# Two attention beginnings in a new order of waits, copies and roundings

## The reference

```python
def mla_mixer(xn, w_in, q_norm, w_uq, kv_norm, w_ukv, w_o, cos_r, sin_r):
    c = xn @ w_in                                    # 384 + 256 + 32 columns
    cq = rms_norm_2(c[..., :384], q_norm)            # query latents: 3 tiles of 128
    ckv = rms_norm_2(c[..., 384:640], kv_norm)       # key/value latents: 2 tiles
    kr = c[..., 640:]                                # one rotated key part for all heads
    qf = (cq @ w_uq).reshape(B, S, 16, 64 + 32)
    q_rope = apply_rope(qf[..., 64:], cos_r, sin_r)
    kv = (ckv @ w_ukv).reshape(B, S, 16, 64 + 64)
    k_rope = broadcast(apply_rope(kr))
    o = causal_attention(concat(qf[..., :64], q_rope), concat(kv[..., :64], k_rope), kv[..., 64:])
    return o.reshape(B, S, 1024) @ w_o
```

## Time and profile before

| | |
|---|---|
| median of the runs | 1141.34 us (1139.76 to 1141.94, 3 runs) |
| the profiled execution | 1140.0 us, span of its instructions 1138.2 us |
| PE busy | 1113.8 us, 98% of the span |
| DVE, ACT, POOL busy | 872.7, 712.6 and 88.8 us |
| mean granted TensorE clock | 0.993 of full speed; 1.00 in both stretches of the change |
| second attention with its values | about 548 to 640 us of the span |
| latent attention, from its latents on | about 843 to 945 us |

### The profile page before, as it was taken

The page is one execution under the profiler, slowest core; times in us unless marked ns, Lnnn a source line. Parts: engine busy times, 40 slices in busy tenths (PEclk is TensorE's granted clock), DMA queues, the critical chain, the costliest instruction groups (busy, mean ns, idle before and its releaser), DMA issues.

```text
span 1138.2 us, 25181 instructions
## 1 busy us (share of the span) xinstructions
PE 1113.8 (98%) x9391; PEld 1076.8 (95%) x9391; DVE 872.7 (77%) x1640; ACT 712.6 (63%) x1296; POOL 88.8 (8%) x141
## 2 busy tenths in 40 slices
PE   9998999999999999999989999999999999999997
PEld 8998999988999999999889999999998889999997
DVE  6888878686578998888778588777777858876774
ACT  7768764476646666655699476555565836655553
POOL 0000000065200000000023100000001420000000
PEclk9998999999999999999999999999999999999999
DMA  7665645531373776666545357666653425776661
GB/s 250 195 207 185 185 126 164 170 112 57 91 207 130 208 225 195 191 195 186 166 150 148 101 158 221 206 192 195 190 153 102 130 87 164 214 217 191 194 192 37
DMA packets 52780, 190.28 MB, mean 167 GB/s; under 512 B 5984, under 2 KB 6240, under 8 KB 52704
## 3 DMA queue, kind: packets, MB, share of 16 engines
q1 hardware_dynamic: 52272, 188.11, 54.5%
q10 hardware_dynamic: 432, 1.12, 0.3%
HBM read 188.16 MB, written 1.05 MB: 166 GB/s over the span
## 4 chain that ended last, share of the span: by engine, by line
PE 85%; DVE 5%; ACT 5%; DMA 2%; issue 2%; SPq 0%; DVEq 0%; ACTq 0%
PE bank L619 25%; PE bank L621 24%; PE bank L620 24%; PE bank L738 2%; DMA w_raw<-weight_stream 2%; DVE w_low L1804 2%; PE bank L750 2%; ACT w_high L1301 1%; PE bank L627 1%; PE bank L629 1%; PE bank L628 1%; PE bank L767 1%; ACT h_high L1344 1%; ACT arena L1661 1%; PE bank L765 1%
## 5 line engine op out<-in xcount | busy, mean ns | idle before, releaser
L1301 ACT ACTIVATE w_high<-w_raw 128x1024 fp32r<-128x1024 f32 x355 | 374.1, 1059 | 262.6 <-PE bank L621 169.5
L1804 DVE TENSOR_TENSOR w_low<-w_raw,w_high 128x1024 fp32r<-128x1024 f32 x355 | 433.0, 1223 | 132.0 <-ACT w_high L1301 130.2
L619 PE MATMUL bank<-h_high,w_high 128*128 128x256 f32 x1760 | 494.4, 281 | 1.0 <-DVE w_low L1804 0.4
L621 PE MATMUL bank<-h_high,w_low 128*128 128x256 f32 x1760 | 487.4, 277 | 0.0
L620 PE MATMUL bank<-h_low,w_high 128*128 128x256 f32 x1760 | 487.4, 277 | 0.0
L619 PEld LDWEIGHTS bank<-h_high,w_high 128*128 128x128 f32 x1760 | 331.2, 188 | 6.2 <-issue 2.1
L620 PEld LDWEIGHTS bank<-h_low,w_high 128*128 128x128 f32 x1760 | 330.9, 188 | 0.0
L621 PEld LDWEIGHTS bank<-h_high,w_low 128*128 128x128 f32 x1760 | 330.6, 188 | 0.0
L619 PE MATMUL bank<-r_high,w_high 128*128 128x256 f32 x942 | 268.0, 285 | 9.3 <-DVE arena L1866 2.9
L620 PE MATMUL bank<-r_low,w_high 128*128 128x256 f32 x942 | 262.5, 279 | 0.0
L621 PE MATMUL bank<-r_high,w_low 128*128 128x256 f32 x942 | 262.4, 279 | 0.0
(11 more groups left out here) (224 smaller groups left out, 1071.9 us busy)
## 6 DMA issues: line engine op xcount, KB each, us to landing
w_raw<-weight_stream SPq DMA_DIRECT2D x355, 512.0 KB, 4.0
x<-x_in SPq DMA_DIRECT2D x4, 256.0 KB, 5.6
small<-small_in ACTq DMA_DIRECT2D x1, 937.5 KB, 4.7
out<-arena SPq DMA_DIRECT2D x3, 256.0 KB, 2.3
out<-arena SPq DMA_DIRECT2D x1, 128.0 KB, 2.5
out<-arena ACTq DMA_DIRECT2D x1, 128.0 KB, 2.6
small<-small_in ACTq DMA_DIRECT2D x1, 30.5 KB, 4.1
```

The lines of the kernel that those rows point to most:

```text
L619: mm(out_ap, wh, high, start=start, stop=False, skip_group_check=True)
L621: return mm(out_ap, wl, high, start=False, stop=stop, skip_group_check=True)
L1301: fn(w_high[:, c % RING, :], w_raw[:, c % RAW, :], ACT.Copy).then_inc(high_ready, 1)
L1804: v.tensor_tensor(w_low[:, c % RING, :], w_raw[:, c % RAW, :], f(w_high[:, c % RING, :]), ALU.subtract).then_inc(low_ready, 1)
```

## The change

It changes the order of instructions on PE, ACT and DVE, and adds one instruction:

- Second attention: the load of Exp's table moves from behind the value stage to ahead of it, right behind `roots(2)`. The rounding of the chunk six behind the last value chunk moves from ahead of the first `rope_halves` to behind it, and each of the next ones one item later (`behind=1`); behind the third item two are rounded. DVE's low halves follow the same order.
- Latent attention, PE: the wait for the last latent tile's copy moves from ahead of the value stage to behind its first six matmuls (`inside_values`).
- DVE: `turn_key` moves ahead of `latent_inverse(0)`. Of the four `values_out`, number 0 goes to ACT, behind the first two key copies; a new semaphore `first_values` orders it, and `acc_read` gets two counts from the last copy of DVE.
- ACT: a dummy loads Exp's table ahead of `query_copy(0)`; the chunks `ukq`+4 and +5 are rounded behind `query_copy(0)` and `query_copy(2)`, ahead of all exponents, and on DVE at heads 0 and 1 of the attention.
- `LATENT_SPLITS` is now one chunk a block: `ukq`+6+q at head 2q+1 on ACT and 2q+2 on DVE.
- Each dummy of a table load writes a column of its own in `stats`.

```diff
@@ -383,6 +383,7 @@
         c_rstd_ready = sem("latent_rstd_ready")
         c_spread = sem("latent_rstd_spread")
         c_normed = sem("latent_normed")
+        first_values = sem("first_quarter_of_values_copied")
         k2_ready = sem("mla_rotated_keys_spread")
         keys_done = sem("mla_key_products")
         queries_done = sem("mla_query_products")
...
@@ -459,16 +460,7 @@
                 eng.wait_ge({"k": keys_done, "q": queries_done}[kind],
                             sum(not ends_chunk(kind, j) for j in range(i + 1)))
-        def latent_splits():
-
-            out, at = collections.defaultdict(list), -1
-            for q in range(-SIZE["uv"], SIZE["ukq"]):
-                kind, i, _ = UNITS[max(8 * q + 7, 0)]
-                at = max(at + 1, 2 * i - 3 if kind == "k" else i - QUERIES_AHEAD)
-                out[at].append(BASE["ukq"] + q + RING)
-            return out
-
-        LATENT_SPLITS = latent_splits()
+        LATENT_SPLITS = {2 * q: BASE["ukq"] + q + RING for q in range(SIZE["ukq"])}
         QK_AHEAD = 3
...
@@ -1188,12 +1180,12 @@
                         latent_root_spread(1)
             column_tiles("c2", h_high, h_low, inside=inside_latents, norm=4)
-            tile_read(pe, "c2", 5)
             pe.wait_ge(std_ready, 5)
             pe.wait_ge(c_normed, 2)
             def inside_values(k, t):
                 if (k, t) == (0, 0):
+                    tile_read(pe, "c2", 5)
                     latent_norm_sums(0)
                 if (k, t) == (1, 0):
                     latent_root_spread(0)
...
@@ -1258,8 +1250,10 @@
             def queries_keys_and_bank(h):
                 queries_and_keys(h)
-                if h < 2:
-                    pe.wait_ge(acc_read, 4 * ACC_V2 + 2 + h)
+                if h == 0:
+                    pe.wait_ge(first_values, 1)
+                if h == 1:
+                    pe.wait_ge(acc_read, 4 * ACC_V2 + 2)
             for m in range(2):
                 key_product(m)
...
@@ -1638,21 +1632,21 @@
             stage("wo", lambda i: None, DT - LATE)
             norm(1)
             late_splits(BASE["ffn0"], LATE)
-            fn(stats[:, 6:7], eps_col, ACT.Sqrt)
+            fn(stats[:, 9:10], eps_col, ACT.Sqrt)
             feed_forward(0)
             norm(2)
             late_splits(BASE["v1"], LAG)
             roots(2)
+            fn(stats[:, 10:11], eps_col, ACT.Exp)
             stage("v1", lambda i: None, SIZE["v1"] - 1)
             act.wait_ge(chunk_used, BASE["v1"] + SIZE["v1"])
             for p in range(4):
                 read_acc(p, v1[:, p // 2, (p % 2) * 512:(p % 2 + 1) * 512], scale=rstd_col[:, p // 2:p // 2 + 1])
-            split_high(BASE["v1"] + SIZE["v1"] - 1 + RING)
-
-            def rope_halves(n):
+
+            def rope_halves(n, behind=0):
                 act.wait_ge(chunk_used, BASE["qk1"] + n + 1)
                 if n >= 2:
                     act.wait_ge(rope_done, n - 1)
...
@@ -1661,11 +1655,12 @@
                     ins = fn(rope_swap[at:at + HD // 2, n % 2, :], qk_bank(n)[other:other + HD // 2, :], ACT.Copy,
                              scale=qk_scale(n))
                 ins.then_inc(halves_swapped, 1)
-                split_high(BASE["qk1"] + n + RING)
-
-            fn(stats[:, 7:8], eps_col, ACT.Exp)
+                split_high(BASE["qk1"] + n - behind + RING)
+
             for n in range(QK_AHEAD):
-                rope_halves(n)
+                rope_halves(n, behind=1)
+            split_high(BASE["qk1"] + QK_AHEAD - 1 + RING)
+
             def behind_block(j, part):
                 n = QK_AHEAD + 2 * j + part
...
@@ -1731,8 +1726,13 @@
             for m in range(2):
                 key_copy(m)
-            for h in range(QUERIES_AHEAD):
+            fn(v2[:, 0, 0:512], acc[0][:, :], ACT.Copy).then_inc(first_values, 1)
+            fn(stats[:, 15:16], eps_col, ACT.Exp)
+            query_copy(0)
+            split_high(BASE["ukq"] - SIZE["uv"] + RING)
+            for h in range(1, QUERIES_AHEAD):
                 query_copy(h)
+            split_high(BASE["ukq"] - SIZE["uv"] + 1 + RING)
             def inside_latent(j):
...
@@ -1746,16 +1746,15 @@
                     key_copy(j + 2)
                 if part and i + QUERIES_AHEAD < NH:
                     query_copy(i + QUERIES_AHEAD)
-                if i < NH:
-                    for c in LATENT_SPLITS[i]:
-                        split_high(c)
+                if part and i < NH:
+                    split_high(LATENT_SPLITS[i - 1])
             attention(3, NH // 2, probs2, probs_t2, LATER_BANKS, behind_latent, inside_latent, odd_copies=False)
             for k in range(DT - LATE):
                 projection_split("wo2", k)
             norm(5)
             late_splits(BASE["ffn2"], LATE)
-            fn(stats[:, 6:7], eps_col, ACT.Sqrt)
+            fn(stats[:, 13:14], eps_col, ACT.Sqrt)
             feed_forward(2)
             def squared(n):
...
@@ -2246,7 +2245,7 @@
             inverse_roots(2)
             v.tensor_tensor(c64r, par("c64"), rstd[:, :], ALU.mult)
             link(v.tensor_tensor(s64r, par("s64"), rstd[:, :], ALU.mult))
-            stage("v1", lambda i: None)
+            stage("v1", lambda i: None, count=SIZE["v1"] - 1)
             def rope(n):
                 dve.wait_ge(halves_swapped, n + 1)
...
@@ -2255,7 +2254,12 @@
                 link(v.tensor_tensor(b, rope_swap[:, n % 2, :], s64r, ALU.mult))
                 dve.wait_ge(qk_read, n + 1)
                 v.tensor_tensor((k1[:, 0, n // 2, :] if n % 2 else q1[:, n // 2, :]), a, b, ALU.add).then_inc(rope_done, 1)
-                split_low(BASE["qk1"] + n + RING)
+                if n < QK_AHEAD - 1:
+                    split_low(BASE["qk1"] + n - 1 + RING)
+                else:
+                    if n == QK_AHEAD - 1:
+                        split_low(BASE["qk1"] + n - 1 + RING)
+                    split_low(BASE["qk1"] + n + RING)
             def projection_split(name, k):
...
@@ -2323,14 +2327,14 @@
                 if i == 1:
                     latent_inverse(1)
                     inverse_roots(4)
+            turn_key()
             latent_inverse(0)
-            turn_key()
             latents_normed(0, 2, 5)
             split_low(BASE["c2"] + SIZE["c2"] - 1 + RING)
             dve.wait_ge(chunk_used, BASE["uv"] + SIZE["uv"])
-            def values_out(p):
-                v.tensor_copy(v2[:, p // 2, (p % 2) * 512:(p % 2 + 1) * 512], acc[p][:, :]).then_inc(acc_read, 1)
+            def values_out(p, banks=1):
+                v.tensor_copy(v2[:, p // 2, (p % 2) * 512:(p % 2 + 1) * 512], acc[p][:, :]).then_inc(acc_read, banks)
             def query_rope(h):
                 product_done(dve, "q", h)
...
@@ -2340,18 +2344,20 @@
             values_out(2)
             query_rope(0)
             query_rope(1)
-            values_out(0)
             values_out(1)
             query_rope(2)
-            values_out(3)
+            dve.wait_ge(first_values, 1)
+            values_out(3, banks=2)
             def behind_latent(j, part):
                 i = 2 * j + part
                 if i + QUERIES_AHEAD < NH:
                     query_rope(i + QUERIES_AHEAD)
-                for c in LATENT_SPLITS[i - 2]:
-                    split_low(c)
+                if i < SIZE["uv"]:
+                    split_low(BASE["ukq"] - SIZE["uv"] + i + RING)
+                if i - 2 in LATENT_SPLITS:
+                    split_low(LATENT_SPLITS[i - 2])
             attention(3, NH // 2, probs_t2, LATER_BANKS, behind_latent, odd_copies=True)
             for k in range(DT - LATE):
```

More of the change, by code:

```diff
@@ L1413, in step @@
                         roots(2 * n + 1)
-                        fn(stats[:, 7:8], eps_col, func)
+                        fn(stats[:, 44 + n:45 + n], eps_col, func)
                     if j:
@@ L1456, in _ @@
             split_high(3)
-            fn(stats[:, 6:7], eps_col, ACT.Sqrt)
+            fn(stats[:, 7:8], eps_col, ACT.Sqrt)
             split_high(4)
@@ L1529, in _ @@
             rx(RT - 1)
-            fn(stats[:, 6:7], eps_col, ACT.Sigmoid)
+            fn(stats[:, 8:9], eps_col, ACT.Sigmoid)
             def branch_gates():
@@ L1684, in _ @@
             late_splits(BASE["ffn1"], LATE)
-            fn(stats[:, 6:7], eps_col, ACT.Sqrt)
+            fn(stats[:, 11:12], eps_col, ACT.Sqrt)
             feed_forward(1)
@@ L1704, in latents_high @@
                     fn(r_high[:, LATENTS[n], :], c_norm[:, LATENTS[n], :], ACT.Copy).then_inc(latent_high, 1)
-            fn(stats[:, 6:7], eps_col, ACT.Sqrt)
+            fn(stats[:, 12:13], eps_col, ACT.Sqrt)
             for i, e in enumerate(C2_ORDER):
@@ L1769, in weighted @@
                 ins.then_inc(out_scaled, 1)
-            fn(stats[:, 6:7], eps_col, ACT.Sqrt)
+            fn(stats[:, 14:15], eps_col, ACT.Sqrt)
             squared(0)
```

## The result

The changed kernel takes 1134.12 us in the median of 6 runs (1132.91 to 1138.09), the kernel before 1141.01 us beside it (6 runs, 1139.76 to 1142.29): a ratio of 0.995 with a 95% interval of 0.9938 to 0.9962. Timed once more it was 1133.36 against 1139.58 us, ratio 0.995 (0.9934 to 0.9967). Forecast was 1135.1. The profiled execution of the changed kernel took 1134.8 us, with a span of 1133.0.

A forecast was written before the change was run, and what follows sets the result against it. PE was taken as the bound, so only its waits in the two stretches could be won: 1.05 + 5.1 = 6.15 us off 1140.0 gives 1133.8, and the median 1.3 above gives 1135.1; range 1132.3 to 1138.3.

The forecast's parts named there:

- Second attention, 1.05: Second attention: earlier table load and later roundings bring ACT's first exponents forward, winning 1.05 us of 3.7 to be had.
- The values, "1.0 us won": Latent attention: the values' first products start at 861.05 instead of 862.03, before the last tile's copy, winning 1.0 us.
- Low half 2 against POOL's fourth copy: Latent attention: DVE's low half (868.24) gets in before POOL's copy (868.27), so query 0 starts at 870.7, 1.6 us earlier.
- rival 1: Latent attention: POOL's fourth copy gets in ahead of DVE; 5.1 us won in all, 1136.2 us; chance 0.21.
- Turning the key early: Latent attention: turning the key inside DVE's idle time starts POOL's four copies at 865.0 instead of 867.49.
- First exponents at 876.15: Latent attention: ACT's chain of copies, table load and roundings lets the exponents start at 876.15, 2.25 us earlier.
- Waits left, 2.0: Latent attention: of PE's 7.1 us of waits, 0.85 (query 0), 0.4, 0.1 and 0.65 (query 6) remain; 5.1 won.
- The wait of 1.52: Latent attention: PE's long wait, from ACT stuck 2.09 us on a transfer ahead of exponents, vanishes with earlier rounding.
- The last roundings, "ACT is idle there": Latent attention's end: the last rounding moves back a block at no cost, its chunk wanted over 5 us later.
- Rival 2: Both stretches: the waits vanish nearly whole, DVE's and ACT's slack being larger; 8.8 us, 1132.5; chance 0.12.
- Rival 3: Latent attention: DVE's two low halves push the second block's maxima back; only 2.0 us won, 1139.3; chance 0.14.
- Slower by landing transfers: Second attention: later low halves delay loads; landings near 7 us would cost 8.5 us, giving 1144; chance 0.03.

The follow-up runs named there:

- e1: Kernel before with only the second attention's part of the change: 1136.69 us in one execution.
- e2: Kernel before with only the second attention's load of Exp's table moved ahead of the value stage, roundings as before: 1137.02 us in one execution.
- e3: Changed kernel with PE's wait for the last latent tile's copy put back ahead of the values: 1135.05 us in one execution.
- e8: Changed kernel with POOL's last three key copies held back behind the latents' last low half: 1134.16 us in one execution.
- e4: Changed kernel with the key turned behind the root's reciprocal again, as before: 1138.28 us in one execution.
- e6: Changed kernel with the latent attention's roundings and low halves in the old order: 1135.52 us, beside 1139.77 of before.
- e9: Changed kernel with DVE's low halves spread to one a block, ACT's order unchanged: 1133.37 us in one execution.
- e5: Changed kernel with all four quarters of the values copied by DVE, as before: 1136.37 us, beside 1139.77 of before.
- e7: Changed kernel again without edit, as a control: 1135.83 us in one execution.
- e11: Changed kernel again without edit, timed: median of 6 runs 1133.36 us, against 1139.58 of before.
- e12: Changed kernel with POOL's copies held back, one low half a block, and the second attention's roundings in before's order: median of 5 runs 1132.24 us, against 1139.58.

## Why the prediction was right

The forecast was 6.15 us, 1135.1; medians measured 6.89 and 6.22 us less than before. The stretches show 5.6 to 6.0 us. So the sum is right, within what this kernel's runs can tell, and so is the mechanism in the main: 5.6 to 6.0 us came out of PE's waits in the two stretches (5.2 to 5.8 if e1 and e2 stand for before in the latent one). One step failed, and its cost was offset by luck. The steps:

- **Second attention, 1.05.** Measured 0.97 to 1.08. First wait near 0.1: 0.16. Second about 1.5: 1.58. First exponents at 578.65: 577.50, which is 578.65 on before's clock (1.15 us ahead there). The "0.45 of waiting for PE" that the text took off the table load's 1.5 is what e2 wins back (1.50 against 1.04). The cover was there: ACT waits for no transfer between 565 and 600 us.
- **The values, "1.0 us won".** At the values' first product it is 1.01. As a gain at query 0 it is 0 to 0.4 (e3). The text named the next thing that would be late, POOL's fourth copy, but still counted the 1.0 whole.
- **Low half 2 against POOL's fourth copy.** This step failed. I took DVE to get in first, by 0.03 us; the copy did, and low half 2 took 1.26. The copies started at 864.79 on before's clock, not 865.0, and ran 1.09 apart, so the fourth began some 0.2 us sooner than I had it. That same earliness made the loss smaller than rival 1's: query 0 at 870.77, where the forecast said 870.7 and the rival 871.1. The mechanism was the rival's and the size the forecast's. So query 0's time came out right by luck. The Trainium skill's "SBUF — State Buffer", section "Who interferes with whom", says that a DVE instruction with two SBUF inputs and a reading GpSimd instruction contend, and that the order of issue decides which of them is blocked. The trace agrees: a copy under way holds off DVE's subtraction (1.26 against 0.42), and in e8 a subtraction under way isn't held off by the copy behind it (1.22 at 868.12, the copy drawn from 868.33; the three copies took 4.11 there, where one alone took 1.04).
- **Turning the key early.** Right in kind, and larger than I had weighed it: 2.0 to 2.4 us (e4), since the late copies strike all three low halves and the query chain behind. The text foretold POOL's copies "2.5 us earlier against the values"; by its own times (865.0 and 861.05, before 867.49 and 862.03) it is 1.5, and 1.7 was measured. The 2.5 is their shift on before's clock, measured 2.7.
- **First exponents at 876.15.** 876.45 on before's clock. ACT's key copies began at 870.17 and not 869.6, because its last rounding waited for DVE behind low half 2. From there to the exponents it took 6.28 us and not 6.55: successive copies and roundings are drawn overlapping by some 0.1 us (the rounding behind query copy 0, 1.05 us long from 871.91, is followed at 872.86), which the count left out. The text built this time on ACT's chain alone; by e6 DVE's maxima would not have let the exponents start before 876.46 either. That both bounds fall together is nothing that the text had worked out.
- **Waits left, 2.0.** From start to start of the matmuls, less what such a step takes without a wait, PE loses 1.0 us at query 0 (forecast 0.85), 0.2 at the first head's scores (none), 0.4 at the second head's (0.4), nothing at query 4 (0.1) and 0.7 at query 6 (0.65): 2.3. With the text's own 7.1 that makes 4.8, and the profile has 4.77. So 7.1 was right and the 2.0 was 0.3 short. The 0.2 is most likely query copy 0, which now stands behind the table load and ends at 872.01, PE going on at 872.22; the view names no cause. As idle time query 0's wait is 0.86, where about 0.7 was foretold.
- **The wait of 1.52** is gone, for the reason given (e6).
- **The last roundings, "ACT is idle there".** The text put them at nothing. The rest of the attention loses 0.15 us in the three executions of the changed kernel and in every experiment with its order of roundings, and not in e1, e2 and e6, which have before's order (0.04, 0.04 and -0.01 us gained).
- **Rival 2** (8.8 us) wasn't reached even with three repairs (7.96). **Rival 3**, given back: no; e9 shows that the two low halves cost 0.8 to 0.9 us, and the second block's exponents behind them start at 879.69 (881.81 on before's clock) where before had 883.25. **Slower by landing transfers:** no. Landings have a median of 4.2 us (4.0 in the earlier trace rows), and the second attention gained 1.0 of its 1.05.

**Open.** Behind the latent attention, from its output projection into the feed-forward, every execution loses 0.15 to 1.6 us against before's one profile, e1 and e2 among them (0.81 and 0.41), whose latent attention is unchanged. So it isn't shown to be the change's. Why the medians gain 0.2 to 1.1 us more than the stretches of the profile taken with them (6.22 against 5.97, 6.89 against 5.81) is open too; single runs of one kernel differ by 2 us and more.

## What to carry to other kernels

Where two engines shut one another out, moving one engine's work earlier is worth what the other's timetable leaves of it: find what is queued in the gap that the chain moves into, and test the two edits together and apart, since each alone may win little (here 0 to 0.4 us apart, 1.0 together). A table load moved to a place where its engine has cover was worth its whole 1.5 us here; a rounding moved away from the head of a chain partly uncovered the wait that it was hiding (0.4 to 0.5 us). Before shortening one engine's chain ahead of a step, ask which other engine that step also waits for: here ACT could take two roundings more ahead of the first exponents for nothing, since DVE's maxima weren't there sooner. If work is made ahead for one engine, ask which engine now has the matching half to do and spread that too.

## What the runs showed of the hardware

In a series of four copies of POOL the gap ahead of the last one was no opening for DVE. By the copies' even spacing (4.35 us for four) the last one began about 0.1 us before low half 2 was drawn, in the changed kernel, in e5 and in e6, and in all three low half 2 took 1.26 us in place of 0.42.

Two executions ran the same products at two paces with the same clock. Windows of 7 us in the latent attention's output projection, of before and then of the changed kernel; columns are length, busy time and count of PE, PEld, DVE, ACT and POOL, granted clock, DMA share, GB/s:

```profile
933.00:940.00 7.00, 7.00 (x64) 7.00 (x63) 4.18 (x4) 2.90 (x3) 0.00 (x0) 1.00 0.57 181
```

```profile
926.40:933.40 7.00, 7.00 (x62) 7.00 (x61) 3.83 (x4) 2.76 (x3) 0.00 (x0) 1.00 0.54 173
```

64 and 62 products touch these 7 us, and by their starts they follow each other 0.113 and 0.118 us apart, with PE never idle and the clock at 1.00 in both. It isn't the kernel: e7 and e11, the changed kernel again, ran these products 0.113 us apart, and e2, e5, e9 and e12 0.118. Over 60 products that makes 0.3 us. The cause is open.
